# A two-block fp32 transformer kernel: operand order in the matmul blocks, panels that end tile by tile, and new leads behind two norms

## The chip, the cores and the metric

One core of a Trainium2 chip runs the whole program. The metric is the device time of one execution in microseconds (us); lower is better. The engines: TensorE (PE in the profile; PEld is its weight load), VectorE (DVE), ScalarE (ACT), GpSimd (POOL) and the sync engine (SP), which issues the DMAs of the weights.

## What is computed

Two networks follow each other on 256 tokens of width 2048, all in fp32: a block with adaLN modulation, four kinds of attention and a SwiGLU, then two layers with a mixer, a cross-attention to a memory and a layer norm.

```python
def first_block(x, c, ...):
    mod = silu(c) @ ada_w + ada_b                       # sh1, sc1, g1, sh2, sc2, g2
    u = rms_norm(x, g_mix) * (1 + sc1) + sh1
    h = x + g1 * hybrid_mixer(u, w_in, ..., w_out)
    u = rms_norm(h, g_ffn) * (1 + sc2) + sh2
    h = h + g2 * ((silu(u @ w_gate) * (u @ w_up)) @ w_down)
    return rms_norm(h, final_g)

def second_block(h, mem, w_in, w_out, w_mem_kv, ln_g, ln_b, ...):
    for i in range(2):
        u = h @ w_in[i]                                 # i == 1: and h @ w_kv_shared
        mixed = gate(mixer_i(u), memory_attention(u, mem))
        h = layer_norm(ALPHA * h + mixed @ w_out[i], ln_g[i], ln_b[i])
    return h
```

## The kernel before

**Products.** An fp32 product is made of three in the faster format fp32r: with `x = hi + lo` for both operands, `hi*w_hi + hi*w_lo + lo*w_hi`. The activations (`actT`, `hidT`, `mixT`) lie transposed and split in SBUF and are the stationary operand, 128x128 at a time; the weights stream through as the moving one, 512 columns wide. A **block** is one K block of 128 rows of weights for both row tiles of 128 tokens (t = 0, 1): six matmuls, L550 to L552, tile 0's three into one PSUM bank and then tile 1's three into the next:

```python
for t in range(T):
    ...
    nc.tensor.matmul(o, hi, w_hi[:, g, 0:w], ...)
    nc.tensor.matmul(o, hi, w_lo[:, g, 0:w], ...)
    last = nc.tensor.matmul(o, lo, w_hi[:, g, 0:w], ...)
last.then_inc(parts_used, 1)
```

A **panel** is 512 output columns over all K, mostly 16 blocks. The stages in order are `memkv`, `win_k`, `win`, `wout` (first block), `gu0`, `down0`, `gu1`, `down1`, `gu2`, `down2` (SwiGLU), `in0`, `out0`, `in1`, `out1` (the two layers): 1,328 blocks, 7,968 such matmuls.

**Streams.** SP loads pairs of K blocks into a ring `raw` of eight slots and goes on when VectorE has read them (semaphore `blocks_read`). ScalarE rounds a block to `w_hi` (L434) in a ring of `HILO` = 4 slots as soon as TensorE has finished the block four before (`parts_used`); VectorE makes `w_lo = raw - w_hi` (L481) when `hi_ready` says so; TensorE waits for `blocks_read`, that is for `w_lo`, ahead of each block. The order on every engine is written out by hand: `lead`, `hooks`, `at` and `each` are tables from the K block (or a running number) to the other work that is put ahead of this block: attention, accumulation of the adaLN product on VectorE (L460), copies from PSUM.

**Joints.** Where a norm needs all columns of the sum, the last panel of a stage is followed by a chain without products. After `wout`: VectorE multiplies by the gate (`gated_out`, L2142), adds to `X` (L2150), takes statistics (L1944), aggregates and finishes them (`moments`, L1933 to L1938); GpSimd raises to -1/2 (`inv_sqrt`, L1225); ScalarE scales the rows (`normalise`, L1711) by quarters of the width; TensorE transposes them (`turning`, L583; one *turn* is two K blocks, four transposes, eight turns in all, four ahead of the stage and four within it); VectorE scales and shifts (`mod`, L657) into `evac`, ScalarE rounds it to the high part (`high`, L623), VectorE subtracts for the low part (`low`, L664). Meanwhile TensorE runs eleven idle matmuls (`keep_running`, L1348). On VectorE and ScalarE this lead stands behind the first four blocks' `w_lo` and `w_hi` (`in_lead`: `lead[4] = first`), the later turns `g` at K block 2g. After `out0` it is the same with `layer_out` (L2372) and `normalise("l0", X)` in place (L1708). After `out1` comes the end: VectorE subtracts the mean and multiplies by the gain (L2396), then scales and adds the shift (L2400), by halves of the width and row tiles, and SP stores four pieces (L1152).

## Time and profile before

| | |
|---|---|
| median of 3 runs | 2149.55 us (2147.91 to 2149.69) |
| the profiled execution, its own time | 2144.39 us |
| its span, first to last instruction | 2142.7 us |
| mean granted TensorE clock | 0.994 of full speed |
| busy: TensorE, VectorE, ScalarE, GpSimd | 97%, 67%, 50%, 4% |
| DMA over the span | 468.88 MB, 219 GB/s |

The profile is of one execution; its times are its own, and starts are counted from the span's beginning. Matmuls are pipelined and their ends are modelled, so distances between starts say more than their durations. An fp32 transpose or idle matmul is recorded as two passes. In square brackets behind a row stands the idle time of the engine just before it and what ended it.

### The profile page before, as it was taken

The numbers are of one execution on the slowest core, as the hardware profiler recorded it, in microseconds if no ns is written. First come the engines' busy times: TensorE is split into PE (matmuls) and PEld (weight loads), VectorE is DVE, ScalarE is ACT, GpSimd is POOL, SyncE is SP. The second block draws the span as 40 slices with busy tenths as digits, with TensorE's granted clock in tenths as the row PEclk, the third lists the DMA queues.
The fourth block names the chain that finished last, engine by engine and source line by source line (L and its number), as shares of the span: only waits on it lengthen the run. The fifth ranks groups of instructions, "written<-read, shape, count | busy, mean of one in ns | idle before, by whom it ended". The sixth has DMA issues, their size and how long they took to land.

```text
span 2142.7 us, 28517 instructions
## 1 busy us (share of the span) xinstructions
PE 2082.1 (97%) x9926; PEld 1704.7 (80%) x9926; DVE 1428.3 (67%) x2489; ACT 1065.0 (50%) x1955; POOL 86.7 (4%) x156
## 2 busy tenths in 40 slices
PE   6999999999999999999999999999999999999996
PEld 5787788887877887888888888788788788888885
DVE  5987798799577786555555556854455655455556
ACT  3644455555445444445444454454454555555542
POOL 2000011110030000000000000000000000000000
PEclk9999999999999999999999999999999999999998
DMA  8999788888647886666666665664466455555562
GB/s 308 367 366 318 246 289 298 274 292 277 225 157 256 276 291 220 196 194 186 189 191 194 191 187 186 202 211 138 151 214 195 141 156 176 176 160 172 171 225 90
DMA packets 281466, 468.88 MB, mean 219 GB/s; under 512 B 17120, under 2 KB 111552, under 8 KB 279936
## 3 DMA queue, kind: packets, MB, share of 16 engines
q1 hardware_dynamic: 278576, 451.32, 65.1%
q0 software_dynamic: 2768, 15.98, 2.2%
q8 instruction: 71, 1.16, 0.2%
q14 instruction: 51, 0.42, 0.1%
HBM read 465.13 MB, written 2.10 MB: 218 GB/s over the span
## 4 chain that ended last, share of the span: by engine, by line
PE 87%; DVE 5%; issue 5%; ACT 1%; DMA 1%; SPq 0%; POOL 0%; DVEq 0%; POOLq 0%; ACTq 0%
PE ps L550 26%; PE ps L552 25%; PE ps L551 25%; DVE w_lo L481 1%; PE ps L796 1%; PE ps L768 1%; PE ps L1348 1%; PE ps L1633 1%; PE ps L996 1%; PE ps L974 1%; DVE acc_a L460 1%; PE ps L509 1%; PE ps L780 1%; ACT w_hi L434 1%; DMA X<-in_x 1%
## 5 line engine op out<-in xcount | busy, mean ns | idle before, releaser
L481 DVE TENSOR_TENSOR w_lo<-raw,w_hi 128x512 fp32r<-128x512 f32 (+1 forms) x1328 | 901.5, 689 | 646.3 <-ACT w_hi L434 641.2
L434 ACT ACTIVATE w_hi<-raw 128x512 fp32r<-128x512 f32 (+1 forms) x1328 | 830.7, 629 | 989.6 <-PE ps L552 956.3
L550 PE MATMUL ps<-w_hi,actT 128*128 128x512 f32 (+2 forms) x1920 | 771.7, 402 | 11.1 <-DVE w_lo L481 7.1
L552 PE MATMUL ps<-w_hi,actT 128*128 128x512 f32 (+2 forms) x1920 | 747.6, 389 | 0.0
L551 PE MATMUL ps<-w_lo,actT 128*128 128x512 f32 (+2 forms) x1920 | 745.8, 388 | 0.0
L550 PEld LDWEIGHTS ps<-w_hi,actT 128*128 128x128 f32 x1920 | 361.2, 188 | 94.1 <-DVE w_lo L481 10.8
L552 PEld LDWEIGHTS ps<-w_hi,actT 128*128 128x128 f32 x1920 | 361.0, 188 | 76.5
L551 PEld LDWEIGHTS ps<-w_lo,actT 128*128 128x128 f32 x1920 | 361.7, 188 | 69.5 <-issue 1.4
L550 PE MATMUL ps<-w_hi,hidT 128*128 128x512 f32 x352 | 138.4, 393 | 3.0 <-DVE w_lo L481 3.0
L552 PE MATMUL ps<-w_hi,hidT 128*128 128x512 f32 x352 | 137.1, 390 | 0.0
L551 PE MATMUL ps<-w_lo,hidT 128*128 128x512 f32 x352 | 137.0, 389 | 0.0
L550 PE MATMUL ps<-w_hi,mixT 128*128 128x512 f32 x256 | 100.2, 392 | 1.5 <-DVE mixT L2310 1.5
L551 PE MATMUL ps<-w_lo,mixT 128*128 128x512 f32 x256 | 99.6, 389 | 0.0
L552 PE MATMUL ps<-w_hi,mixT 128*128 128x512 f32 x256 | 99.6, 389 | 0.0
L460 DVE SCALAR_TENSOR_TENSOR acc_a<-raw,c_col,acc_a 128x1024 f32<-128x1024 f32 x75 | 97.9, 1305 | 2.1 <-DVE acc_a L460 0.5
L550 PEld LDWEIGHTS ps<-w_hi,hidT 128*128 128x128 f32 x352 | 66.1, 188 | 18.5 <-DVE w_lo L481 2.8
L552 PEld LDWEIGHTS ps<-w_hi,hidT 128*128 128x128 f32 x352 | 66.1, 188 | 13.9
L551 PEld LDWEIGHTS ps<-w_lo,hidT 128*128 128x128 f32 x352 | 66.1, 188 | 13.3
L550 PE MATMUL ps<-w_hi,memT 128*128 128x512 f32 x128 | 52.0, 406 | 12.1 <-DVE memT L614 8.6
L550 PEld LDWEIGHTS ps<-w_hi,mixT 128*128 128x128 f32 x256 | 48.1, 188 | 12.2 <-DVE mixT L2310 2.3
L552 PEld LDWEIGHTS ps<-w_hi,mixT 128*128 128x128 f32 x256 | 48.1, 188 | 10.1
L551 PEld LDWEIGHTS ps<-w_lo,mixT 128*128 128x128 f32 x256 | 48.1, 188 | 9.7
(290 smaller groups left out, 1589.6 us busy)
## 6 DMA issues: line engine op xcount, KB each, us to landing
raw<-in_w_in SPq DMA_DIRECT2D x208, 512.0 KB, 4.5
raw<-in_ada_w SPq DMA_DIRECT2D x192, 512.0 KB, 5.3
raw<-in_w_out SPq DMA_DIRECT2D x96, 512.0 KB, 4.2
raw<-in_ffn_w_gate SPq DMA_DIRECT2D x176, 256.0 KB, 2.9
raw<-in_ffn_w_up SPq DMA_DIRECT2D x176, 256.0 KB, 3.1
...
```

The source lines that it names most:

```text
L434: act.activation(w_hi[:, g, 0:w], raw[:, slot_of(st, it), b, 0:w], ACT.Copy).then_inc(hi_ready, 1)
L460: ins = nc.vector.scalar_tensor_tensor(acc[:, :], both, c_col[:, it.ch:it.ch + 1], acc[:, :], ALU.mult, ALU.add)
L481: nc.vector.tensor_tensor(w_lo[:, g, 0:w], raw[:, slot, b, 0:w], w_hi[:, g, 0:w].bitcast(f32), ALU.subtract).then_inc(blocks_read, 1)
L509: last = nc.tensor.matmul(ps[:, bank, i:i + 1], acc[:, i * P:(i + 1) * P], ones[:, 0:1], start=True, stop=True)
L550: nc.tensor.matmul(o, hi, w_hi[:, g, 0:w], start=first_k, stop=False)
L551: nc.tensor.matmul(o, hi, w_lo[:, g, 0:w], start=False, stop=False)
L552: last = nc.tensor.matmul(o, lo, w_hi[:, g, 0:w], start=False, stop=last_k)
L768: last = nc.tensor.matmul(ps[:, 5 + h, c0:c0 + nk], q[:, t * P:(t + 1) * P], k[:, 0:nk], start=True, stop=True)
L780: last = nc.tensor.transpose(ps[0:self.keys, 5 + h, d:d + P], probs[:, self.par, h, c0 + kt * P:c0 + kt * P + self.keys], ident[:, :])
L796: last = nc.tensor.matmul(o, probsT[0:self.keys, h, d:d + P], self.v(kt, h), start=(kt == 0), stop=(kt == nk // self.keys - 1))
L974: last = nc.tensor.matmul(ps[:, 6 + h, c0:c0 + nk], pair_qkT[:, h, 0, t * P:(t + 1) * P], pair_qkT[:, h, 1, 0:nk], start=True, stop=True)
L996: last = nc.tensor.matmul(o, self.pT[:, h, d:d + P], self.v(kt, h), start=(kt == 0), stop=(kt == nk // P - 1))
```

## The change

- `stage_matmuls`: the six matmuls of a block go by operand: `w_hi` with the high parts of both tiles, `w_hi` with the low parts, then `w_lo` with the high parts. The block now waits for `hi_ready`, and only the fifth matmul for `blocks_read`. With `tiles_apart` (`wout`, `out0`, `out1`) the last four blocks of the last panel are held: all their products for tile 0 come first, then `tile_done`, then all for tile 1.
- VectorE's work behind these three panels goes tile by tile (`last_out`, `layer_out`, `tile_moments`), tile 0's behind `tile_done`.
- Leads of `u2` (into `gu0`) and `h1` (into `in1`): VectorE makes the first two turns' rows itself (`first_rows`); two turns ahead of the stage in place of four, six within it; K blocks 0 and 1 get their high and low parts one by one (`first_hi`, `first_low`). VectorE's lead now stands ahead of its first `w_lo`, and its later steps are `mod(g)` at K block 2g and `low(g)` at 2g + 1. Idle matmuls: 7 and 5 in place of 11 and 11.
- GpSimd builds the pooling masks (`band`) only when the eight turns of `u2` are done. Ahead of `l0`'s `nmean`, `rinv` is signalled.
- The end: tile 0's first half is centred (mean off, gain on) while the panel ends; power for each tile apart; five stores, the last two half as wide (256 KB).

TensorE, one block in a loop (`gu1`), before:

```order
L543 REGISTER_ALU
L550 MATMUL ps<-w_hi,actT 128x512 [waits blocks_read]
L551 MATMUL ps<-w_lo,actT 128x512
L552 MATMUL ps<-w_hi,actT 128x512
L550 MATMUL ps<-w_hi,actT 128x512
L551 MATMUL ps<-w_lo,actT 128x512
L552 MATMUL ps<-w_hi,actT 128x512
```

and with the change:

```order
L559 REGISTER_ALU
L533 MATMUL ps<-w_hi,actT 128x512 [waits hi_ready]
L533 MATMUL ps<-w_hi,actT 128x512 x3
L565 REGISTER_ALU
L533 MATMUL ps<-w_lo,actT 128x512 [waits blocks_read]
L533 MATMUL ps<-w_lo,actT 128x512
```

The two products with `w_lo` have moved behind the other four, and there are two waits in place of one.

VectorE from the norm behind `wout` into `gu0`, before (`evac` is scaling and shifting, `actT` the low part):

```order
L1938 TENSOR_SCALAR ms<-ms 128x2
L481 TENSOR_TENSOR w_lo<-raw,w_hi 128x512 x4
L657 TENSOR_SCALAR evac<-ps,gain,modT 128x256 x4
L664 TENSOR_TENSOR actT<-evac,actT 128x512
L657 TENSOR_SCALAR evac<-ps,gain,modT 128x256 x2
L664 TENSOR_TENSOR actT<-evac,actT 128x512
L481 TENSOR_TENSOR w_lo<-raw,w_hi 128x512 x2
L657 TENSOR_SCALAR evac<-ps,gain,modT 128x256 x2
L664 TENSOR_TENSOR actT<-evac,actT 128x512
L481 TENSOR_TENSOR w_lo<-raw,w_hi 128x512 x2
```

and with the change:

```order
L2009 TENSOR_SCALAR ms<-ms 128x2
L2046 TENSOR_SCALAR xn_68<-X,rinv_x 128x256 x4
L732 TENSOR_SCALAR evac<-ps,gain,modT 128x256 x2
L737 TENSOR_TENSOR actT<-evac,actT 128x256 x2
L481 TENSOR_TENSOR w_lo<-raw,w_hi 128x512 x2
L710 TENSOR_SCALAR evac<-ps,gain,modT 128x256 x2
L481 TENSOR_TENSOR w_lo<-raw,w_hi 128x512
L717 TENSOR_TENSOR actT<-evac,actT 128x512
L481 TENSOR_TENSOR w_lo<-raw,w_hi 128x512
L710 TENSOR_SCALAR evac<-ps,gain,modT 128x256 x2
L481 TENSOR_TENSOR w_lo<-raw,w_hi 128x512
```

The four `w_lo` ahead of the lead are gone from there, the rows are new, and the low part stands between the two `w_lo` of a pair. On ScalarE the high part of a pair still stands ahead of the pair's `w_hi`.

VectorE at the end of the program, before:

```order
L2372 SCALAR_TENSOR_TENSOR X<-X,ps 128x512 x2
L1952 BN_STATS stats<-X 128x6 x2
L1933 BN_AGGR mv<-stats 128x2 x2
L1940 TENSOR_SCALAR ms<-mv 128x2
L2396 SCALAR_TENSOR_TENSOR X<-X,mv,gb_77 128x1024 x2
```

and with the change:

```order
L2502 SCALAR_TENSOR_TENSOR X<-X,ps 128x512
L2028 BN_STATS stats<-X 128x6
L2032 BN_AGGR mv<-stats 128x2
L2517 TENSOR_SCALAR ms<-mv 128x1
L2534 SCALAR_TENSOR_TENSOR X<-X,mv,gb_77 128x1024
L2502 SCALAR_TENSOR_TENSOR X<-X,ps 128x512
```

Tile 0's five steps have moved ahead of tile 1's first. The diff, cut to its core:

```diff
         def stage_matmuls(pe, name, lhs, hooks=None, width=None, as_columns=False, one_acc=False, lead=None, at=None,
-                          sum_at=8, carry=False, each=None):
+                          sum_at=8, carry=False, each=None, tiles_apart=False, between=None):
...
+                held = st.items[-2:] if tiles_apart and (st.bodies == 1 or not first) else []
+
+                def products(it, b, tiles, which):
+
+                    g, kk = (it.g + b) % HILO, 2 * st.place[it.ch] + b
+                    w = width[it.j] if width else NC
+                    first_k, last_k = it is st.first[it.j] and b == 0, it is st.last[it.j] and b == 1
+                    for t in tiles:
+                        last = nc.tensor.matmul(ps[:, bank_of(st, it.j) + t, 0:w], lhs[:, int(which == 1), kk, t * P:(t + 1) * P],
+                                                (w_hi, w_hi, w_lo)[which][:, g, 0:w], start=first_k and which == 0,
+                                                stop=last_k and which == 2)
+                    return last
...
+                        tiles = range(1) if it in held else range(T)
+                        pe.wait_ge(hi_ready, at_p.gb + it.g + b + 1)
+                        products(it, b, tiles, 0)
+                        if between and k in between and first and it.j == 0:
+                            between[k]()
+                        products(it, b, tiles, 1)
+
                         pe.wait_ge(blocks_read, 2 * RING + at_p.kb + it.off + b + 1)
-                        g = (it.g + b) % HILO
-                        for t in range(T):
-                            kk = 2 * st.place[it.ch] + b
-                            hi, lo = (lhs[:, part, kk, t * P:(t + 1) * P] for part in range(2))
-                            first_k, last_k = it is st.first[it.j] and b == 0, it is st.last[it.j] and b == 1
-                            o = ps[:, bank + t, 0:w]
-                            nc.tensor.matmul(o, hi, w_hi[:, g, 0:w], start=first_k, stop=False)
-                            nc.tensor.matmul(o, hi, w_lo[:, g, 0:w], start=False, stop=False)
-                            last = nc.tensor.matmul(o, lo, w_hi[:, g, 0:w], start=False, stop=last_k)
-                        last.then_inc(parts_used, 1)
+                        last = products(it, b, tiles, 2)
+                        if it not in held:
+                            last.then_inc(parts_used, 1)
+                if held:
+                    last.then_inc(S("tile_done"), 1)
+                    for it in held:
+                        for b in range(2):
+                            for which in range(3):
+                                last = products(it, b, (1,), which)
+                            last.then_inc(parts_used, 1)
             run_bodies(pe, st, body)
...
+        def turning_early(pe, src, ready, tag):
+
+
+            def turn(g):
+                ready(g)
+                for i in range(4):
+                    k, t = 2 * g + i // 2, i % 2
+                    last = nc.tensor.transpose(ps[:, 4 + g % 4, i * P:(i + 1) * P], src(k, t), ident[:, :])
+                last.then_inc(turned, 1)
+
+            def taken(g):
+                pe.wait_ge(turn_taken, TURNS[tag] + g + 1)
+
+            def both(g, other):
+                taken(g)
+                turn(other)
+            turn(0)
+            turn(1)
+
+            def second():
+                taken(0)
+                turn(2)
+            n = 1 if tag == "u2" else 3
+            return {0: lambda: pe.wait_ge(S("first_hi"), n), 1: second, 2: lambda: both(1, 3), 4: lambda: both(2, 4), 6: lambda: both(3, 5),
+                    8: lambda: both(4, 6), 10: lambda: both(5, 7), 12: lambda: taken(6), 14: lambda: taken(7)}, {
+                        0: lambda: pe.wait_ge(S("first_low"), n)}
...
+            high = high_of(act, tag, dst)
+
+            def first():
+                n = 2 * ("u2", "h1").index(tag)
+                for k in range(2):
+                    act.wait_ge(S("first_mod"), n + k + 1)
+                    last = act.activation(dst[:, 0, k, :], evac[:, 0, k * SEQ:(k + 1) * SEQ], ACT.Copy)
+                    last.then_inc(S("first_hi"), 1)
+                act.sem_inc(turn_hi, 1)
+                quarter(1)
+                quarter(2)
+                high(1)
+
+            def later(g):
+                if g == 3:
                     quarter(3)
-                high_g(g)
-
-            def first():
-                if quarter:
-                    quarter(0)
-                    quarter(1)
-                high(0)
-                high(1)
-                if quarter:
-                    quarter(2)
-                high(2)
-            return in_lead(first, high)
+                high(g)
+            lead = in_lead(first, later)
+            lead[5] = lambda: high(2)
+            return lead

...
             mod, low = mod_low_of(dve, tag, dst, gain_of, shift_of)

             def first():
-                mod(0)
-                mod(1)
-                low(0)
-                mod(2)
-                low(1)
-
-            def later(g):
-                mod(g)
-                low(g - 1)
-            lead = in_lead(first, later)
-            lead[15] = lambda: low(7)
+                rows_of(0)
+                rows_of(1)
+                n = 2 * ("u2", "h1").index(tag)
+                dve.wait_ge(turned, TURNS[tag] + 1)
+                half = [slice(k * SEQ, (k + 1) * SEQ) for k in range(2)]
+                for k in range(2):
+                    nc.vector.tensor_scalar(evac[:, 0, half[k]], ps[:, 4, half[k]], gain_of(k), shift_of(k), ALU.mult,
+                                            ALU.add).then_inc(S("first_mod"), 1)
+                dve.sem_inc(turn_mod, 1)
+                for k in range(2):
+                    dve.wait_ge(S("first_hi"), n + k + 1)
+                    nc.vector.tensor_tensor(dst[:, 1, k, :], evac[:, 0, half[k]], dst[:, 0, k, :].bitcast(f32),
+                                            ALU.subtract).then_inc(S("first_low"), 1)
+                dve.wait_ge(S("first_low"), n + 2)
+                dve.sem_inc(turn_taken, 1)
+            lead = {2 * g: (lambda g=g: mod(g)) for g in range(1, 8)}
+            lead.update({2 * g + 1: (lambda g=g: low(g)) for g in range(1, 8)})
+            lead[0] = first
             return lead

...
+            pool.wait_ge(turn_taken, TURNS["u2"] + 8)
...
-            stage_matmuls(pe, "wout", actT, each=beside_mixer)
...
-            keep_running(11, 4)
-            lead = turning(pe, "u2", lambda k, t: xn2[:, t, k * P:(k + 1) * P], quarter_ready("u2"))
+            stage_matmuls(pe, "wout", actT, each=beside_mixer, tiles_apart=True)
+
+            keep_running(7, 4)
+            lead, between = turning_early(pe, lambda k, t: xn2[:, t, k * P:(k + 1) * P], quarter_ready("u2"), "u2")
...
+            def tile_moments(q, t, tag):
+
+                ins = v.bn_stats(stats[:, t, q, :], X[:, t, q * NC:(q + 1) * NC])
+                if t == 0:
+                    ins.then_inc(S("tile_stats"), 1)
+                    dve.wait_ge(S("tile_stats"), ("n2", "l0", "l1").index(tag) + 1)
+                    ins = v.bn_aggr(mv[:, 0, :], stats[:, 0, :, :].rearrange("p a b -> p (a b)"))
+                    if tag == "l1":
+                        ins.then_inc(S("tile_mv"), 1)
+                else:
+                    ins.then_inc(S("panel_stats"), 1)
+
+            def first_rows(tag, dst):
+
+                def rows_of(g):
+                    if g == 0:
+                        dve.wait_ge(S("rinv"), NORM[tag])
+                    for t in range(T):
+                        cs = slice(2 * g * P, 2 * (g + 1) * P)
+                        if tag == "n2":
+                            ins = v.tensor_scalar(dst[:, t, cs], X[:, t, cs], rinv_x[:, t:t + 1], None, ALU.mult)
+                        else:
+                            ins = v.tensor_scalar(dst[:, t, cs], X[:, t, cs], mv[:, t, 0:1], rinv_x[:, t:t + 1],
+                                                  ALU.subtract, ALU.mult)
+                    ins.then_inc(S("xn_first"), 1)
+                return rows_of
...
+            def last_out():
+
+                st, cs = ST["wout"], slice(3 * NC, 4 * NC)
+                dve.wait_ge(S("row_taken"), 4)
+                dve.wait_ge(S("panel_stats"), 4 + 3)
+                for t in range(T):
+                    if t == 0:
+                        dve.wait_ge(S("tile_done"), 1)
+                    else:
+                        panel_done(dve, st, 0, 3)
+                    ins = v.tensor_tensor(gy_odd[:, t, :], ps[:, bank_of(st, 3) + t, :], g1_row[:, cs], ALU.mult)
+                    if t == 1:
+                        ins.then_inc(acc_read, 1)
+                        dve.wait_ge(acc_read, 2 + st.end[2])
+                    else:
+                        ins.then_inc(S("tile_gated"), 1)
+                        dve.wait_ge(S("tile_gated"), 1)
+                    v.tensor_tensor(X[:, t, cs], X[:, t, cs], gy_odd[:, t, :], ALU.add).then_inc(S("gy"), 1)
+                    dve.wait_ge(S("gy"), 3 + t + 1)
+                    tile_moments(3, t, "n2")
+            last_out()
...
+                for t in range(T):
+                    if t == 0:
+                        dve.wait_ge(S("natural"), 4 * n)
+                        dve.wait_ge(S("tile_done"), 1 + n)
+                        dve.wait_ge(S("panel_stats"), 4 * NORM[tag] - 1)
+                    else:
+                        panel_done(dve, st, 1, 1)
+                    ins = v.scalar_tensor_tensor(X[:, t, cs], X[:, t, cs], ALPHA, ps[:, bank_of(st, 1) + t, :],
+                                                 ALU.mult, ALU.add)
+                    if t == 1:
+                        ins.then_inc(acc_read, 1)
+                        dve.wait_ge(acc_read, 2 + st.end[2])
+                    else:
+                        ins.then_inc(S("tile_added"), 1)
+                        dve.wait_ge(S("tile_added"), n)
+                    tile_moments(3, t, tag)
+                    if tag == "l1":
+                        if t == 1:
+                            dve.wait_ge(S("panel_stats"), 4 * NORM[tag])
+                            v.bn_aggr(mv[:, 1, :], stats[:, 1, :, :].rearrange("p a b -> p (a b)")
+                                      ).then_inc(S("tile_mv"), 1)
+                        dve.wait_ge(S("tile_mv"), t + 1)
+                        v.tensor_scalar(ms[:, t:t + 1], mv[:, t, 1:2], LN_EPS, None, ALU.add).then_inc(S("ms"), 1)
+                        if t == 0:
+                            while_panel_ends()
+                if tag == "l0":
+                    moments(tag, LN_EPS, False)

...
-                cs = slice(half * D // 2, (half + 1) * D // 2)
-                for t in range(T):
...
-                                           ALU.mult, ALU.add).then_inc(S("y_done"), 1)
+                final(0, slice(half * D // 2, (half + 1) * D // 2))
+            centred(1, slice(0, D // 2))
+            chain(centred(1, slice(D // 2, D)))
+            dve.wait_ge(S("rinv"), NORM["l1"] + 1)
+            for t, cs in OUT_PIECES[2:]:
+                final(t, cs)
```

## Rows read from the trace of the kernel before

**Rows 1.** the page, busy time of each engine
```profile
PE 2082.1 (97%) x9926; PEld 1704.7 (80%) x9926; DVE 1428.3 (67%) x2489; ACT 1065.0 (50%) x1955; POOL 86.7 (4%) x156
```

**Rows 2.** timeline, TensorE in `gu1`: start us, us, engine, line, operation
```profile
1000.54 0.39 PE L551 MATMUL ps<-w_lo,actT 128*128 128x512 f32 x1
1000.77 0.39 PE L552 MATMUL ps<-w_hi,actT 128*128 128x512 f32 x1
1001.00 0.39 PE L550 MATMUL ps<-w_hi,actT 128*128 128x512 f32 x1
```

**Rows 3.** waits of the whole run: us in total, times, longest
```profile
PEld ps L550 <- DVE w_lo L481: 18.3, 24, 2.4
```

**Rows 4.** stretches: us; busy PE, PEld, DVE, ACT, POOL; PEclk, DMA share, GB/s
```profile
55.00:160.00 105.00, 100.88 (x470) 82.69 (x468) 95.26 (x127) 54.93 (x94) 1.09 (x1) 1.00 1.02 366
...
230.00:232.00 2.00, 2.00 (x6) 1.33 (x5) 2.00 (x4) 0.00 (x0) 0.00 (x0) 0.50 0.95 313
...
476.00:515.00 39.00, 34.89 (x231) 29.07 (x229) 38.52 (x105) 23.30 (x69) 3.56 (x3) 1.00 0.81 272
```

**Rows 5.** timeline, TensorE where it waited for `w_lo`
```profile
229.69 0.62 PE L550 MATMUL ps<-w_hi,actT 128*128 128x512 f32 x1 [1.94 <-DVE w_lo L481]
230.11 0.63 PE L551 MATMUL ps<-w_lo,actT 128*128 128x512 f32 x1
...
510.09 0.47 PE L550 MATMUL ps<-w_hi,actT 128*128 128x512 f32 x1 [1.45 <-DVE w_lo L481]
...
1323.93 0.50 PE L550 MATMUL ps<-w_hi,hidT 128*128 128x512 f32 x1 [0.51 <-DVE w_lo L481]
```

**Rows 6.** timeline, the joint from `wout` to `gu0`
```profile
615.78 7.26 PE L1348 MATMUL ps<-cmask,ident 128*128 128x384 f32 x22
...
616.08 1.29 DVE L2142 TENSOR_TENSOR gy_odd<-ps,g_row 128x512 f32<-128x512 f32 x2 [4.18 <-PE ps L552]
...
620.05 0.39 DVE L1933 BATCH_NORM_AGGREGATE mv<-stats 128x2 f32<-128x24 f32 x2
...
620.93 2.49 DVE L481 TENSOR_TENSOR w_lo<-raw,w_hi 128x512 fp32r<-128x512 f32 x4
621.12 1.08 POOL L1225 TENSOR_TENSOR rinv_x<-ms,mhalf 128x2 f32<-128x2 f32 x1 [51.85 <-DVE ms L1938]
...
622.23 2.56 ACT L1711 ACTIVATE xn<-X,rinv_x 128x512 f32<-128x512 f32 x4 [5.63 <-POOL rinv_x L1225]
...
626.92 0.47 PE L550 MATMUL ps<-w_hi,actT 128*128 128x512 f32 x1 [0.98 <-issue]
```

**Rows 7.** timeline, TensorE at `out0`'s end, then one pair of blocks of `in1`
```profile
1674.47 0.48 PE L1348 MATMUL ps<-cmask,ident 128*128 128x384 f32 x1
...
1693.04 0.99 DVE L657 TENSOR_SCALAR evac<-ps,cols 128x256 f32<-128x256 f32 x2
...
1695.25 1.29 DVE L481 TENSOR_TENSOR w_lo<-raw,w_hi 128x512 fp32r<-128x512 f32 x2 [0.62 <-ACT w_hi L434]
1696.46 0.99 DVE L657 TENSOR_SCALAR evac<-ps,cols 128x256 f32<-128x256 f32 x2
...
1694.07 0.63 ACT L623 ACTIVATE actT<-evac 128x512 fp32r<-128x512 f32 x1 [1.75 <-DVE evac L657]
1694.60 1.14 ACT L434 ACTIVATE w_hi<-raw 128x512 fp32r<-128x512 f32 x2
...
1707.81 0.39 PE L550 MATMUL ps<-w_hi,actT 128*128 128x512 f32 x1
```

**Rows 8.** timeline, VectorE behind the last product
```profile
2125.50 1.28 DVE L2372 SCALAR_TENSOR_TENSOR X<-X,ps 128x512 f32<-128x512 f32 x2 [4.15 <-PE ps L552]
...
2129.64 2.48 DVE L2396 SCALAR_TENSOR_TENSOR X<-X,mv,gb 128x1024 f32<-128x1024 f32 x2 [0.91 <-POOL rinv_x L1225]
...
2137.06 2.48 DVE L2400 SCALAR_TENSOR_TENSOR X<-X,rinv_x,gb 128x1024 f32<-128x1024 f32 x2
```

**Rows 9.** the stores of `out`, issue to landing
```profile
DMA to landing us min/median/max: 2.7/2.7/2.7
```

92 lines of the change are left out of this document (49 added, 43 removed).

## The prediction

> **What bounds the kernel now.** The page says TensorE, 97% busy [rows 1]. Matmuls overlap in that row, so I read the distance between starts in the timeline: 0.227 us for a 512-column product, the same when the next one goes to the other row tile and so to another PSUM bank and another stationary block (1000.77 to 1001.00) as when it doesn't (1000.54 to 1000.77) [rows 2]. A block of six takes 1.36 us. Nothing in the change makes it shorter, so the kernel can win only where TensorE waits. There are four kinds of places.
>
> The list of waits gives 18.3 us in 24 waits of the weight load for `w_lo` [rows 3]. The joints behind `wout` and behind `out0`, where a norm needs the whole panel, cost 11.14 us (615.78 to 626.92) and about as much again: fills and transposes, no products [rows 6, 7]. The first 16 blocks behind a joint run slower than 1.36 us, since VectorE has to scale, shift and split the activations beside them [rows 7]. And the tail, from about 2125.2 (0.3 us ahead of the first VectorE step) to the end at 2142.7, is VectorE work [rows 8].
>
> **Order within a block.** The low weights are now used last. A block may start when `w_hi` is there, and needs `w_lo` four products later, 0.91 us. So each wait for `w_lo` shrinks by at most 0.91. Not all of this counts.
> - Before 190 us the DMA share is 1.02 and VectorE is busy for 95.26 of 105 us [rows 4]; eleven adaLN accumulations in a row pace the program there. I take 0 (bound: 2.5 us, as much as three such waits could give).
> - At 229.69 the wait was 1.94 us [rows 5]. It becomes 1.0: gain 0.9. Behind this wait the granted clock is 0.50 [rows 4] and the starts are 0.42 us apart (229.69 to 230.11) [rows 5], which is the 1.2 GHz level. The shorter pause, with four products in its middle, probably keeps 2.4 GHz: six products by 0.2 us are 1.2, and some 0.4 on the 64 small fp32 ones behind them. Gain 1.6, bounds 0 and 3 (twice the price, if a later fall hangs on this one).
> - From 476 to 515 VectorE is busy for 38.52 of 39 us [rows 4]: it paces everything, and the waits (510.09 is the last of three [rows 5]) are one lag. Gain 0.9, bound 2.6.
> - In `down2` three waits of about 0.66 us beyond the pace (1323.93 is the first [rows 5]: 0.51 idle and the slow start behind it) lie 18 us apart. VectorE idles between, so each goes whole: 2.0.
>
> Sum: 5.4. A second wait per block costs nothing as long as it's met: today's wait sits at every sixth product, and the starts don't show it [rows 2]. If the extra wait or the change of bank at every product did cost, it'd be up to 10 ns (the reading error of these starts) by 7,968 products, 80 us. I take 0, since the change of bank is in the rows at no cost and VectorE is normally blocks ahead.
>
> The Trainium skill (TensorE: Matmul & The Clock Gate, "A second HAM failure mode: psum-queue depth-cycling") reports a kernel that cycles through PSUM banks, where TensorE made tiny pauses and its clock went up and down between the two levels. It speaks against switching the bank with every product. With it the sum would turn positive; the last rival prices that from rows.
>
> **The end of a panel ahead of a norm.** Tile 0's share of the last four blocks runs first (12 products), then tile 1's, 2.72 us. VectorE deals with tile 0 under these 2.72 us and has only tile 1 left. Behind `wout` the three pair operations take 3.97 us (616.08 to 620.05) [rows 6]; half goes, and half of the 0.39 aggregation: 2.1 us less. Behind `out0` it is a multiply-add of 1.28 [rows 8], statistics of 1.3 (a third of the 3.97) and the 0.39 aggregation [rows 6]; half is 1.5. The held blocks need all four `w_hi` slots at twice the pace, but those are filled long before: no new wait. The next panel's `w_hi` slots come free as late as today, at the end.
>
> **The lead into the next stage.** Today: power on GpSimd 1.08, first rows on ScalarE 1.3 (half of 2.56), four turns, scaling, high part, low part, first product at E+11.14, E being the end of the last product [rows 6]. Now VectorE writes the first rows itself in quarters of the width (four pieces of 128x256; above nothing, and at most the 0.5 of the scaling form of that size that reads PSUM [rows 7]; I take 0.3), only two turns precede, and K block 0 starts on its high part alone. Behind `out0`, from E: tile 1's chain ends at 2.0, power 3.2, two pieces 3.8, turn 4.5, scale 5.2, high 5.7, first product at **E+5.8**; behind `wout` **E+6.9**. The shorter fills end at E+3.3 and E+4.6, before the first turn; they hide nothing and cost nothing.
>
> So block 0 is 4 to 5 us earlier. But VectorE used to split four `w_lo` blocks (2.49 us) while GpSimd and ScalarE worked [rows 6]; now its lead starts with the rows, and these four come behind. Turn 2 needs ScalarE's rows of the second quarter, which are made after both high halves: block 1 at E+8.4, block 2 at E+11.0 (E+14.0 before).
>
> From there a chain sets the pace. Today two blocks take scale 1693.04, high 1694.07, `w_hi` 1694.60, `w_lo` twice 1695.25, next scale 1696.46: 3.42 us [rows 7], for VectorE leaves the low part of a group to the next one. The new order has the low part between the two `w_lo`: 1.03 + 0.53 + 0.65 + three steps of 0.605 = **4.03 us**, and TensorE waits at the even block for that low part. Its own need is 2.72 and about 0.5 for four transposes. Stepping the three queues through from block 2, six pairs give 3.3 + 3.6 + 4.0 + 4.0 + 3.5 + 4.0 = 22.5: block 14 at E+33.4 behind `out0`. Before it was 1707.81 - 1674.47 = E+33.34 [rows 7]. Behind `wout` the same comes to E+34.4 against E+34.64 (GpSimd's mask work, now moved behind the lead, stretched VectorE by nearly 1 us). **The two joints together give +0.1, which is nothing**: the front gains 5 and the lead pays it back. Bounds: -4 (0.35 us more per pair) and +7 (the old 3.42 us kept).
>
> **The tail.** Before, VectorE from 2125.50 to 2139.54 (2137.06 + 2.48) [rows 8] and then 2.7 us for 512 KB to land [rows 9]. Now tile 0's multiply-add, statistics, aggregation and one 1024-wide centring (1.2) start at E-2.4 and end at E+0.7. Tile 1: 1.8, to E+2.5. Seven more 1024-wide steps by 1.2 and 0.3 of links: E+11.2, against E+14.3. The power on GpSimd (0.9 us of idle before 2129.64 [rows 8]) is now hidden under centring. The last store is half as large: 0.7 less at the rate of the store today. Gain 3.1 + 0.7 = **3.8**, bounds 2.8 and 4.3.
>
> **Sum:** 5.4 + 0.1 + 3.8 = 9.3. The profiled execution took 2144.39 us (span 2142.7) and would take 2135.1. The median of the runs, 2149.55, is 5.2 above it; I carry the difference over: **2140.3**.
>
> **Rivals.**
> 1. *The lead keeps its old pace*: ScalarE's queue or the early start lets TensorE stay ahead, and the 3 to 4 us won at the front of each joint are kept. For: 5 us at block 0 are sure. Against: the 4.03 us are sums of rows. 7 more: 2133.3.
> 2. *The `w_lo` waits only move*: VectorE is all but full up to 515 us [rows 4], and what TensorE wins is lost at the next attention step; the clock falls all the same. Tail and `down2` stay, 5.8, less a lead that is 1 to 2 us worse: 2145.2, within the limit of measurement. That the change does less than it says falls here.
> 3. *Slower: the clock falls in the lead.* Between the shorter fill and block 2 TensorE has some 5 us with pauses of up to 0.8 us and fp32 transposes between; at 229.69 it fell after 1.94 us idle [rows 5]. At 1.2 GHz a block is 2.5 us, a pair with its turn 5.8 instead of 4.03, 12 us per joint if it stays down for seven pairs. It decides from five such pairs in all (9 us). Both joints down: 2140.3 + 25 = 2165. Against: today's joint has a pause of 0.98 us with only transposes ahead of it [rows 6], and the clock holds.
> 4. *The banks.* If 2% of the products ran 0.42 instead of 0.23 us apart [rows 2, 5]: +32 us, 2172. The mean clock is at its upper level for now at a bank change every third product.
>
> **Numbers.** Forecast 0.64, rival 1 0.12, rival 2 0.17, rival 3 0.05, rival 4 0.02. What a measurement can tell from no change is about 0.2%, 4.3 us. Forecast and rival 1 are faster, rival 2 is the same. Range: the forecast's own bounds are 2136 to 2145; taking in rival 1 and rival 2, 2133.5 to 2146.5.
>
> **What would show it.** First products behind the joints at E+6.9 and E+5.8; evacuation steps (`evac`) 4.0 us apart in the lead, not 3.4; block 14 within 1 us of E+34; no wait over 1.1 us at the 229 us place and a granted clock of 1.00 there; `down2` without its three waits; the last VectorE step 11.2 us behind the last product. Wrong if starts within a block are not 0.227 us apart, if the granted clock falls behind E, or if `evac` steps come at 3.4 us.

## The result, and the profile after

| | before | changed |
|---|---|---|
| median of the runs | 2149.62 us (4 runs) | 2136.21 us (4 runs, 2134.53 to 2138.75) |
| ratio, 95% interval | 1 | 0.9944 (0.9927 to 0.9961) |
| profiled execution, its own time | 2144.39 us | 2135.92 us |
| its span | 2142.7 us | 2133.9 us |

The change is faster, by 13.4 us between these medians and by 8.5 us between the two profiled executions. On the chip of the first experiments, with 12 and 23 runs, the medians were 2135.88 and 2144.43, 8.5 us apart, 0.9955 (0.9939 to 0.9970); a 24th run of before, 2676.3 us at a mean clock of 0.741, is left out. The forecast was 9.3 us and 2140.3.

The page of the changed kernel, busy time of each engine; the row answers to [rows 1]. TensorE has the same share, and GpSimd is 8 us busier for one instruction more:

```profile
PE 2079.7 (97%) x9906; PEld 1705.5 (80%) x9906; DVE 1433.7 (67%) x2502; ACT 1062.1 (50%) x1953; POOL 94.8 (4%) x157
```

The waits of the whole run, changed kernel (us, times, longest), against [rows 3]: half as many, but the longest is hardly shorter.

```profile
PEld ps L533 <- DVE w_lo L481: 11.7, 12, 2.2
```

Next I laid both traces side by side by stage. A stage starts at its first weight product; E is the end of the last product ahead of a norm. In us:

| piece | before | before, 2nd trace | changed | changed, 2nd trace |
|---|---|---|---|---|
| start to E of `wout` | 615.78 | 620.77 | 612.59 | 616.41 |
| `gu0` with its lead, and `down0` | 285.86 | 285.90 | 285.91 | 285.98 |
| `gu1` to `gu2` | 397.93 | 397.93 | 397.90 | 397.91 |
| `down2` and `in0` | 285.75 | 285.58 | 282.84 | 282.86 |
| `out0`, lead, `in1` | 450.71 | 450.81 | 451.04 | 451.02 |
| `out1` | 89.20 | 89.16 | 89.19 | 89.16 |
| from there to the end | 17.47 | 17.45 | 14.43 | 14.36 |

**Read the second and fourth columns first.** Behind E of `wout` two executions of one kernel agree within 0.1 us in total (1526.92 and 1526.83; 1521.31 and 1521.29) and within 0.2 in each piece. Ahead of it they differ by 5.0 and 3.8 us. So a single pair of traces decides about everything behind E, and nothing decides about the first 616 us but many runs.

TensorE in the lead of `gu0`, changed kernel; the idle time before a start stands in brackets:

```profile
612.59 4.68 PE L1415 MATMUL ps<-cmask,ident 128*128 128x384 f32 x14
617.34 1.18 PE L625 MATMUL ps<-ident,xn 128*128 128x128 f32 x8
619.13 1.15 PE L533 MATMUL ps<-w_hi,actT 128*128 128x512 f32 x4 [0.61 <-issue]
...
633.45 0.61 PE L533 MATMUL ps<-w_lo,actT 128*128 128x512 f32 x2
634.68 0.66 PE L625 MATMUL ps<-ident,xn 128*128 128x128 f32 x4 [0.62 <-DVE actT L717]
...
637.49 0.61 PE L533 MATMUL ps<-w_lo,actT 128*128 128x512 f32 x2
638.70 0.65 PE L625 MATMUL ps<-ident,xn 128*128 128x128 f32 x4 [0.60 <-DVE actT L717]
```

The first product stands at E+6.54 (forecast E+6.9, before E+11.14 [rows 6]); behind `out0` it is E+5.53 (forecast E+5.8). Pairs of blocks come 4.04 us apart (633.45 to 637.49), each with 0.6 us of waiting for the low part. Block 14 is at E+34.16 and E+33.16; forecast 34.4 and 33.4. VectorE and ScalarE over one such pair show why:

```profile
631.12 0.99 DVE L710 TENSOR_SCALAR evac<-ps,gain,modT 128x256 f32<-128x256 f32 x2
633.33 0.69 DVE L481 TENSOR_TENSOR w_lo<-raw,w_hi 128x512 fp32r<-128x512 f32 x1 [1.22 <-ACT w_hi L434]
633.94 0.68 DVE L717 TENSOR_TENSOR actT<-evac,actT 128x512 fp32r<-128x512 f32 x1
634.54 0.68 DVE L481 TENSOR_TENSOR w_lo<-raw,w_hi 128x512 fp32r<-128x512 f32 x1
635.15 0.99 DVE L710 TENSOR_SCALAR evac<-ps,gain,modT 128x256 f32<-128x256 f32 x2
...
632.15 0.63 ACT L672 ACTIVATE actT<-evac 128x512 fp32r<-128x512 f32 x1 [2.35 <-DVE evac L710]
632.68 1.14 ACT L434 ACTIVATE w_hi<-raw 128x512 fp32r<-128x512 f32 x2
```

In each such pair VectorE is idle for 1.22 us and ScalarE for 2.35, each waiting for the other: `w_hi` needs nothing of this pair, but stands behind the high part, which waits for the scaling step. That was the pace of 4.03 us in the prediction, and here is also its cure.

### The profile page after: what moved, and what is told of

It is laid out like the page before. It is cut to its first block, busy times and chain, and to the rows that moved or that the text cites. A ratio compares the mean times of both kernels' runs of the same rounds, so it can differ in the third digit from the quotient of the medians.

```text
span 2133.9 us, 28754 instructions
## 1 busy us (share of the span) xinstructions
PE 2079.7 (97%) x9906; PEld 1705.5 (80%) x9906; DVE 1433.7 (67%) x2502; ACT 1062.1 (50%) x1953; POOL 94.8 (4%) x157
## 4 chain that ended last, share of the span: by engine, by line
PE 91%; DVE 6%; ACT 1%; issue 1%; DMA 1%; SPq 0%; POOL 0%; DVEq 0%; ACTq 0%
PE ps L533 80%; DVE w_lo L481 2%; PE ps L856 1%; PE ps L828 1%; PE ps L1415 1%; PE ps L1701 1%; PE ps L1056 1%; PE ps L1034 1%; DVE acc_a L460 1%; PE ps L840 1%; PE ps L509 1%; ACT w_hi L434 1%; DVE ada_acc L493 1%; DMA raw<-in_w_mem_kv 1%; PE ps L1470 0%
## 5 line engine op out<-in xcount | busy, mean ns | idle before, releaser
L533 PE MATMUL ps<-w_hi,actT 128*128 128x512 f32 (+2 forms) x3840 | 1053.4, 396 | 4.3 <-DVE actT L717 3.2
L533 PE MATMUL ps<-w_lo,actT 128*128 128x512 f32 (+2 forms) x1920 | 592.3, 389 | 5.1 <-DVE w_lo L481 5.1
L533 PE MATMUL ps<-w_hi,hidT 128*128 128x512 f32 x704 | 189.6, 391 | 0.0
L533 PE MATMUL ps<-w_hi,mixT 128*128 128x512 f32 x512 | 138.9, 390 | 1.5 <-DVE mixT L2428 1.5
L533 PE MATMUL ps<-w_lo,hidT 128*128 128x512 f32 x352 | 108.6, 390 | 0.5 <-DVE w_lo L481 0.5
L533 PEld LDWEIGHTS ps<-w_hi,memT 128*128 128x128 f32 x256 | 48.4, 192 | 18.8 <-issue 9.0
L493 DVE SCALAR_TENSOR_TENSOR ada_acc<-raw,c_col,ada_acc 128x512 f32<-128x512 f32 x60 | 45.9, 766 | 1.1
L1319 POOL TENSOR_SCALAR tab<-dist 128x384 f32<-128x384 f32 (+1 forms) x34 | 33.8, 999 | 192.0 <-DVE sm L915 191.3
L533 PE MATMUL ps<-w_lo,memT 128*128 128x512 f32 x128 | 40.5, 398 | 1.6 <-DVE w_lo L481 1.4
L460 DVE SCALAR_TENSOR_TENSOR acc_d<-raw,c_col,acc_d 128x1024 f32<-128x1024 f32 x30 | 40.3, 1343 | 0.8 <-DVE acc_d L457 0.5
```

The source lines that it names most:

```text
L460: ins = nc.vector.scalar_tensor_tensor(acc[:, :], both, c_col[:, it.ch:it.ch + 1], acc[:, :], ALU.mult, ALU.add)
L493: nc.vector.scalar_tensor_tensor(acc, raw[:, slot, b, :], c_col[:, k:k + 1], acc, ALU.mult, ALU.add).then_inc(blocks_read, 1)
L533: last = nc.tensor.matmul(ps[:, bank_of(st, it.j) + t, 0:w], lhs[:, int(which == 1), kk, t * P:(t + 1) * P], (w_hi, w_hi, w_lo)[which][:, ...
L1319: last = g.tensor_scalar(to, of, -val / SC, 1.0, ALU.mult, ALU.mult)
```

## The experiments

Twelve kernels ran, two of them without an edit. Ratios are to the kernel before on the same chip.

| kernel | median us | ratio (95%) |
|---|---|---|
| after_again | 2135.88 | 0.9955 (0.9939 to 0.9970) |
| order_only | 2136.89 | 0.9964 (0.9950 to 0.9978) |
| order_and_tiles | 2133.41 | 0.9946 (0.9924 to 0.9969) |
| tiles_short_fills | 2132.53 | 0.9937 (0.9911 to 0.9963) |
| high_later | 2131.54 | 0.9934 (0.9910 to 0.9958) |
| small_spread | 2131.69 | 0.9926 (0.9902 to 0.9950) |
| pause_filled | 2135.65 | 0.9953 (0.9933 to 0.9973) |
| scale_split | 2129.10 | 0.9924 (0.9898 to 0.9950) |
| all_mended | 2119.33 | 0.9876 (0.9853 to 0.9898) |
| before_again, masks_back, masks_in_down0 (one run each) | 2149.32, 2135.68, 2121.74 | |

### The parts of the change, and its leads

**after_again**: no edit.

> The changed kernel itself, so that the parts can be compared on one chip. Theory 1 (the whole gain is waits, joints and tail, as the two profiled executions show: 3.2 us up to the end of wout, 2.9 more up to the end of out0, 3.0 in the tail): 8 to 10 us below the kernel before. Theory 2 (the profiled execution of before was a quick one, and runs differ in the first 515 us, where the DMA share is about 1): 12 to 14 us below.

**order_only**: the diff of `stage_matmuls` alone, without `tiles_apart`.

> The kernel before with the new order of operands alone (high weights with both parts, then low weights, with the two waits). Theory 1 (the wait for w_lo shrinks or goes up to 515 us and in down2, nothing else): 4 to 6 us faster than before, the joints as before (block 14 of gu0 34.6 us behind the end of wout). Theory 2 (the w_lo waits only move): within 2 us of before. Theory 3 (changing the PSUM bank with every product costs): slower.

**order_and_tiles**: this, with tile-by-tile panels and the new end; leads, fills and masks as before.

> The new order of operands, the panels that end tile by tile and the new end of the program, with the old leads, the old fills and GpSimd's masks where they were. Theory 1 (the new leads give their early start back): equal to the whole change within 2 us: the first product of gu0 comes 9 us behind the end of wout and not 6.5, but block 14 about 32.5 us behind it, better than the 34.2 of the whole change. Theory 2 (the new leads are worth their early start of 3 to 4 us per joint): 4 to 8 us slower than the whole change.

Behind E of `wout` the traces give 1526.92 us before, 1523.07 with the order alone, 1518.72 with tiles and end too, 1521.31 for the whole change. The order is worth 3.85 there: 2.5 in `down2`, 0.4 in `in0`, and 1.0 at the start of `down0`. Its median is 7.5 us under before, where 4 to 6 was expected; some 3.7 of it lies ahead of E. The end is worth 3.0. The rest of the change, the leads with their fills and the masks, is **2.6 us slower** than the old leads behind the same panels. So theory 1 on order_and_tiles holds in sign, but its numbers don't: the first product came at E+10.37 and not E+9, block 14 at E+33.8 and not 32.5.

**tiles_short_fills**, on order_and_tiles:

```diff
-            keep_running(11, 4)
+            keep_running(7, 4)
...
-            keep_running(11, 4)
+            keep_running(5, 4)
```

> The kernel with new order and tile-by-tile panels but old leads, now with 7 and 5 idle matmuls in place of 11 and 11. Theory 1 (eleven fills keep TensorE for 7.26 us behind the end of wout and hold the first turn, so that only 0.8 and 0.5 us of the earlier norm arrived): first products at about 9.0 us behind wout (10.37 with the long fills) and 9.3 behind out0 (10.34), 2 to 2.4 us less in all. Theory 2 (the first turn waits for ScalarE's rows anyway): no change. A fall of the granted clock in the lead would speak for a third, that the long fills were needed: 5 us or more slower.

The same place, TensorE in order_and_tiles:

```profile
609.58 7.26 PE L1372 MATMUL ps<-cmask,ident 128*128 128x384 f32 x22
616.68 1.91 PE L605 MATMUL ps<-ident,xn 128*128 128x128 f32 x16
619.95 1.15 PE L533 MATMUL ps<-w_hi,actT 128*128 128x512 f32 x4 [1.36 <-issue]
```

and in tiles_short_fills:

```profile
612.32 4.68 PE L1372 MATMUL ps<-cmask,ident 128*128 128x384 f32 x14
618.14 2.32 PE L605 MATMUL ps<-ident,xn 128*128 128x128 f32 x16 [1.15 <-ACT xn L1735]
621.44 0.93 PE L533 MATMUL ps<-w_hi,actT 128*128 128x512 f32 x3 [0.98 <-issue]
```

With eleven fills the transposes start as the fills end, with no idle time: the fills had become the bound. With seven they wait for ScalarE's rows. First products moved to E+9.12 and E+9.67, the part behind E to 1516.88: 1.8 us less, 4.4 us better than the whole change. Behind `wout` the clock stayed at 1.00. Behind `out0`, with five fills, the fall of the third theory showed in this trace, though not its 5 us:

```profile
1671.37 3.43 PE L605 MATMUL ps<-ident,X 128*128 128x128 f32 x16 [2.78 <-ACT X L1732]
...
1672.00:1673.00 1.00, 1.00 (x7) 0.91 (x6) 0.72 (x2) 0.73 (x2) 0.00 (x0) 0.50 0.88 324
```

Behind an idle time of 2.78 us the granted clock (third column from the end) was 0.50 for some 3.5 us, into the transposes, and the first product came at E+9.67 and not E+9.3. None of the other thirteen traces shows a fall there, also not the changed kernel's with the same five fills in its shorter lead. The number of fills belongs to its lead: too many delay it, too few can, by this one trace, cost the clock.

**high_later**, on the changed kernel: on ScalarE the high part goes behind the pair's first `w_hi`.

```diff
-            def later(g):
-                if g == 3:
-                    quarter(3)
-                high(g)
-            lead = in_lead(first, later)
-            lead[5] = lambda: high(2)
+            lead = {2 * g + 1: (lambda g=g: high(g)) for g in range(2, 8)}
+            lead[4] = first
+            lead[6] = lambda: quarter(3)
```

> The whole change, but on ScalarE the high part of turn g (2 to 7) stands behind the first w_hi of its pair and not ahead of it (and the last quarter of the rows ahead of K block 6). Theory 1 (the 4.02 us per pair in the lead is the chain scale, high part, w_hi, w_lo, low part, w_lo; with w_hi made earlier VectorE no longer idles 1.22 us per pair): the scaling steps come 3.3 us apart, block 14 at 30.6 us behind the end of wout (34.2 in the changed kernel) and 29.7 behind out0 (33.2), 7 us faster than the whole change. Theory 2 (a slot of the ring or the transposes set the pace): the steps stay 4.0 us apart, no gain.

VectorE, then TensorE, in high_later:

```profile
632.50 0.99 DVE L707 TENSOR_SCALAR evac<-ps,gain,modT 128x256 f32<-128x256 f32 x2
633.40 0.69 DVE L481 TENSOR_TENSOR w_lo<-raw,w_hi 128x512 fp32r<-128x512 f32 x1
634.19 0.69 DVE L714 TENSOR_TENSOR actT<-evac,actT 128x512 fp32r<-128x512 f32 x1
634.80 0.69 DVE L481 TENSOR_TENSOR w_lo<-raw,w_hi 128x512 fp32r<-128x512 f32 x1
635.40 0.99 DVE L707 TENSOR_SCALAR evac<-ps,gain,modT 128x256 f32<-128x256 f32 x2
...
632.70 0.60 PE L625 MATMUL ps<-ident,xn 128*128 128x128 f32 x4
633.05 1.18 PE L533 MATMUL ps<-w_hi,actT 128*128 128x512 f32 x4
...
635.90 0.60 PE L625 MATMUL ps<-ident,xn 128*128 128x128 f32 x4
```

No brackets are left: VectorE takes 2.90 us per pair (3.3 was expected) and TensorE its own 3.20. Block 14 is at E+29.93 and E+28.93, 4.2 us earlier at each joint; behind E of `wout` 1512.52, **8.8 us** less than the changed kernel. The median shows 4.3 of it; its six runs had a mean clock of 0.9915 (0.9926 in after_again), and its trace had 615.08 ahead of E, where the edit changes nothing.

### GpSimd's masks, and the start of `down0`

The leads gained 0.34 us by block 16 and `down0`'s start about 1.0, yet `gu0` with `down0` is no shorter. I looked for the missing 1.4.

**masks_back**, on the changed kernel:

```diff
-            pool.wait_ge(turn_taken, TURNS["u2"] + 8)
```

> The whole change, but GpSimd builds the pooling masks without waiting for the eight turns of u2. Theory 1 (behind the lead the masks slow VectorE down and cost 1.4 us in gu0, seen as waits for w_lo of 0.5 and 0.2 us at 57 and 60 us behind the end of wout): those waits go; VectorE's steps in the lead stretch, one pair takes 0.5 to 1 us longer, and gu0 with down0 takes 0.4 to 0.9 us less than the 285.9 of the changed kernel. Theory 2 (the masks are free behind the lead and the 1.4 us have another cause): the waits stay, gu0 with down0 takes up to 1 us longer.

**masks_in_down0**, on high_later; the last adaLN row also goes behind `down0`'s second `w_lo`:

```diff
-            pool.wait_ge(turn_taken, TURNS["u2"] + 8)
+            pool.wait_ge(ada_taken, 1 + ST["gu0"].end[3])
```

> The kernel with high parts behind the first w_hi, and the masks on GpSimd only once the adaLN rows are all added (the start of down0), and this last addition behind down0's second w_lo. Theory 1 (the masks cost 1.4 us in gu0 as long as they run beside its full VectorE, and nothing in down0; the wait of 1.0 for w_lo at the start of down0 is that addition): gu0 and down0 together 279.2 us (281.6 with the high parts later alone, 285.9 in the changed kernel), no wait for w_lo at 57 to 60 us behind wout or at down0's start. Theory 2 (masks cost the same wherever they are): 280.6.

The changed kernel, 57 us behind E of `wout`, GpSimd, VectorE, TensorE:

```profile
664.10 6.86 POOL L1357 TENSOR_TENSOR band<-band,ident 128x128 f32<-128x128 f32 x8
...
666.22 1.82 DVE L481 TENSOR_TENSOR w_lo<-raw,w_hi 128x512 fp32r<-128x512 f32 x2
667.96 1.82 DVE L493 SCALAR_TENSOR_TENSOR ada_acc<-raw,c_col,ada_acc 128x512 f32<-128x512 f32 x2
...
670.70 0.73 PE L533 MATMUL ps<-w_lo,actT 128*128 128x512 f32 x2 [0.48 <-DVE w_lo L481]
```

and VectorE in masks_in_down0 at the same place of the program:

```profile
657.03 1.29 DVE L481 TENSOR_TENSOR w_lo<-raw,w_hi 128x512 fp32r<-128x512 f32 x2
658.24 1.53 DVE L493 SCALAR_TENSOR_TENSOR ada_acc<-raw,c_col,ada_acc 128x512 f32<-128x512 f32 x2
```

Two `w_lo` take 1.82 us beside the masks and 1.29 without, two accumulations 1.82 and 1.53. The Trainium skill (GPSIMD Engine Reference, "1. Specifications") says that GpSimd's way to SBUF is shared with VectorE, whose instructions with two SBUF inputs contend with it; both forms here have two, and the trace agrees. In masks_back the waits in `gu0` go (1.4 us back), but the lead grows by 1.8 (block 16 at E+38.80 in place of E+37.02): 286.32 in all, 0.4 more than the changed kernel and not less, so theory 1 had the mechanism and the wrong balance. In masks_in_down0 the sum is 279.42 (expected 279.2), 2.2 less than high_later: 1.45 for the masks, 0.75 for the start of `down0`. **Moving the masks behind the lead was right, and not far enough.**

### The clock ahead of E

**before_again**: no edit.

> The kernel before once more, for a second trace of its first 616 us, which differ from run to run. Theory 1 (the granted clock falls once or twice there, at a different phase in each run, and the rest of the program is fixed): the time from the end of wout to the end of the span is again 1526.9 us within 0.3, and all of the difference lies ahead of it, with the share of time at the lower clock. Theory 2 (the whole program varies): the part behind wout differs by more than 1 us.

Theory 1 held: 1526.83 behind E. Ahead of it 620.77, with two long falls of the granted clock between 227 and 254 us. In 23 runs of before on one chip, time goes with the mean granted clock: spans of 2148.1 to 2150.2 us at 0.990 (seven runs), 2142.1 to 2143.8 at 0.993 (eight), 2136.1 to 2138.2 at 0.996 (three).

Stretches of the changed kernel; columns: us, busy time (count) of PE, PEld, DVE, ACT, POOL, granted clock, DMA share, GB/s:

```profile
224.00:227.00 3.00, 2.33 (x22) 1.97 (x23) 3.00 (x7) 0.63 (x1) 0.00 (x0) 0.81 0.91 301
227.00:230.00 3.00, 3.00 (x31) 3.00 (x31) 2.42 (x4) 0.00 (x0) 0.00 (x0) 0.50 0.91 250
...
491.00:494.00 3.00, 3.00 (x13) 2.96 (x13) 2.96 (x19) 0.47 (x1) 0.00 (x0) 0.50 0.93 329
```

At 224 us the wait for `w_lo` is 1.79 us, not the 1.0 forecast, and the clock falls as before [rows 4, 5]. At 491 it falls where the trace before keeps 1.00. Both were put to a test.

**small_spread**, on the changed kernel: the two groups of 64 small products that follow the wait go in six parts ahead of six K blocks.

```diff
-                for j in range(CMP_LEN):
+                for j in range(11 * part, min(11 * part + 11, CMP_LEN)):
...
-                elif n in (9, 11):
-                    cmp_hidden((n - 9) // 2)
+                elif 7 <= n < 13:
+                    cmp_hidden((n - 7) // 3, (n - 7) % 3)
```

> The whole change, but the two groups of 64 small products (64x64 by 30 columns, some 4 us each at the upper clock) are given out in six thirds ahead of six K blocks, so that no 4 us pass without full blocks. Theory 1 (the clock falls there because of these small products, with or without the wait for w_lo of 1.8 us ahead of them): no stretch with a granted clock of 0.5 between 225 and 250 us, 4 to 5 us faster than the changed kernel, mean clock 0.995. Theory 2 (the wait alone makes it fall): it still falls once for 3 to 10 us behind the wait, gain under 2 us.

**pause_filled**: the changed kernel with three idle matmuls in the wait, the small products as they were.

```diff
                         products(it, b, tiles, 1)
+                        if name == "win" and st.n0 + it.g + b == 8:
+                            for _ in range(3):
+                                nc.tensor.matmul(ps[:, 4, 0:384], ident[:, :], cmask[:, :], start=True, stop=True)
```

> The changed kernel with three idle matmuls (0.66 us each) between the fourth product of K block 8 of win and its wait for w_lo, so that TensorE works through the wait of 1.8 us ahead of the small products, which stay in two groups of 64. Spreading these groups took away the falls of the granted clock and the wait alike; this run parts the two. Theory 1 (the small products make the clock fall): the wait is gone from TensorE's rows, and the clock still falls to 0.5 within 10 us, at least one fall of 3 us or more between 224 and 250 us; mean clock 0.992 to 0.994, time as the changed kernel within 1.5 us. Theory 2 (the wait makes it fall): no granted clock under 1.00 between 222 and 236 us, a mean clock of 0.995 or more, 3 to 5 us faster.

small_spread, the same view:

```profile
227.00:230.00 3.00, 3.00 (x32) 2.42 (x30) 3.00 (x7) 0.58 (x2) 0.00 (x0) 1.00 0.95 319
```

pause_filled, TensorE and then the view by stretches:

```profile
222.35 2.10 PE L566 MATMUL ps<-cmask,ident 128*128 128x384 f32 x6
224.31 0.73 PE L533 MATMUL ps<-w_lo,actT 128*128 128x512 f32 x2
224.98 4.69 PE L1473 MATMUL ps<-cmp_in,w_k 64*64 64x30 f32 x64
...
235.33 4.78 PE L1473 MATMUL ps<-cmp_in,w_v 64*64 64x30 f32 x64
...
227.00:230.00 3.00, 3.00 (x34) 2.94 (x33) 2.05 (x3) 0.00 (x0) 0.00 (x0) 0.64 0.99 300
230.00:233.00 3.00, 3.00 (x10) 2.31 (x10) 0.00 (x0) 0.44 (x1) 0.00 (x0) 0.50 0.98 349
...
239.00:242.00 3.00, 3.00 (x16) 2.55 (x16) 0.00 (x0) 0.00 (x0) 0.00 (x0) 0.50 0.06 21
```

With the products spread, every stretch from 224 to 245 us has 1.00, and so it is in the two other traces with this edit. The time from the start of `win_k` to the first 480-column panel is 254.79 us (259.04 and 261.77 in the two traces of the changed kernel), and six runs have mean clocks of 0.995 and 0.996. But the wait had gone as well.

With the wait filled instead, TensorE is busy for all of every stretch and the clock still falls twice, from 227.8 and from 238.1 us, each time 2.8 us into a group of small products; the second group has neither a wait nor an idle matmul right ahead of it. The median is 2135.65 (on a chip where before took 2144.57), so nothing was gained. So the small products (64x64 weights, 30 columns, 4 us in a row) can make the clock fall by themselves, though not each time: the changed kernel's second group, at 237.24, ran at 1.00. The place at 380 us is of the same kind: 28 short products take 3.5 us there without a wait, and in six of the fourteen traces the clock is 0.50 for 3.4 us from about their end on.

By the traces the wait can do it too. Before, the starts are 0.42 us apart from 229.69 on, right behind the wait [rows 5], and the first small product comes only at 232.38; in before_again, order_only and tiles_short_fills too the fall begins ahead of the small products. So filling the wait doesn't help while the small products stand behind it. The other half, small products spread and the wait kept, was not run. The Trainium skill (TensorE: Matmul & The Clock Gate, "Why this matters for your kernels") advises keeping idle gaps between bursts short. Here the clock fell with no gap in pause_filled.

**scale_split**, on small_spread: two scaling steps on VectorE, 1.23 and 1.29 us in a row from 483.58 us on, right behind an accumulation of 1.28 and ahead of one `w_lo`, are parted: the first moves one K block ahead, with a `w_lo` between them. (The 2.5 in the expectations is both steps together.)

```diff
-                elif n == 132:
+                elif n == 131:
                     subnorm_scale()
+                elif n == 132:
+                    subnorm_gain()
```

> The changed kernel with the small products spread, and VectorE's two scaling steps at 487 us (3.7 us in a row) parted by one w_lo. Theory 1 (the new order gathered the lag into one wait of 1.13 us in the middle of a block, and behind this wait the granted clock falls to 0.5 for some 5 us, which the kernel before did not show): the wait falls below 0.5 us, no granted clock under 1.00 from 476 to 515, that stretch 1.5 to 2 us shorter, 25.7 or less in place of 27.3. Theory 2 (the fall has to do with the short products of the attention there): the wait goes and the clock falls all the same.

In the changed kernel:

```profile
486.60 0.55 PE L533 MATMUL ps<-w_lo,actT 128*128 128x320 f32 x2 [1.14 <-DVE w_lo L481]
487.08 0.63 PE L828 MATMUL ps<-qkT 64*128 64x16 f32 x8
```

In scale_split:

```profile
491.00:494.00 3.00, 3.00 (x24) 2.74 (x23) 3.00 (x7) 1.07 (x4) 0.00 (x0) 1.00 0.93 333
```

This wait is gone, no stretch from 140 to 620 us is under 1.00, and the 27.3 us from the first 320-column panel to `wout` became 25.08. But `wout` itself took 0.8 longer, and TensorE now waits elsewhere: 1.48 us for ScalarE's `proj` at 475.78 and 1.01 us for `w_lo` at 499.45, inside `wout`. The gain also depends on what it is held against. In five of the ten traces with the new order and the old scaling the fall lasts 3.4 us and not 6.8, and then the same stretch takes 25.7 us and `wout` 0.3 longer, which leaves the edit 0.1 us; against the long fall it is 1.4. Theory 1 fits in that wait and fall went together, but the cause isn't shown: before has a wait of 1.71 us there without a fall, all ten traces with the new order and a wait of 1.1 have one, and scale_split's own 1.48 and 1.01 bring none.

### All together

**all_mended** joins high_later, masks_in_down0 and scale_split, with one `w_lo` ahead of VectorE's rows (`lead[1] = first`).

> The whole change with all that the earlier runs point to: high parts behind the pair's first w_hi (4.1 and 4.4 us fewer per joint), one w_lo ahead of the rows on VectorE, the small products in six thirds, the masks on GpSimd during down0, the last row of the adaLN product added behind down0's second w_lo, and VectorE's scaling of the differential heads (1.2 + 2.5 us in a row ahead of one w_lo at 487 us) in two pieces with a block between. Theory 1 (these are separate costs that add): behind the end of wout 1509.9 us (1521.3 in the changed kernel), ahead of it 607 (612.6), so a span of 2117 and 15 to 18 us faster than the changed kernel, 24 to 28 faster than before. Theory 2 (what is won ahead is lost to the next wait, as between operand order and clock): under 12 us faster than the changed kernel.

Its span is 2117.7 us: 607.16 ahead of E (expected 607; scale_split's one trace had 604.10), 1510.54 behind (expected 1509.9). The median is 2119.33, 16.6 us under the changed kernel's 2135.88, which was measured on another chip (before took 2145.35 and 2144.43 on the two), and 1.2% under before on its own. The `w_lo` ahead of the rows gained nothing: block 16 at E+32.51 (32.65 in high_later) and E+31.98 (31.65).

## Why the prediction was right, and where it was not

Behind E of `wout` the span fell by 5.61 us, forecast 5.9 (2.0 + 0.1 + 3.8). Ahead of E by 3.19 in the pair of profiled executions, forecast 3.4. The total lies close, 8.5 us of time and 8.8 of span against 9.3, but its second part is in part luck: the two second traces differ there by 4.36, and the medians leave 2.9 us for it where they are 8.5 apart and 7.8 where they are 13.4 apart. Of the terms these hold and fail:

- **Nothing within a block.** Held: where nothing waits, blocks start 1.36 us apart in the new order too, as here in `out1` (changed kernel, TensorE):

```profile
2109.95 1.07 PE L533 MATMUL ps<-w_hi,mixT 128*128 128x512 f32 x4
2110.86 0.62 PE L533 MATMUL ps<-w_lo,mixT 128*128 128x512 f32 x2
2111.31 1.07 PE L533 MATMUL ps<-w_hi,mixT 128*128 128x512 f32 x4
```

  Rival 4, the change of bank, is refuted: with a switch at every product the clock stayed at 1.00 from 650 us to the last product. The Trainium skill (TensorE: Matmul & The Clock Gate, "A second HAM failure mode: psum-queue depth-cycling") tells of small pauses that came with cycling through banks. No such pauses showed here, so the switch by itself brought nothing of the kind. (Rival 4's price was a little off too: 2% of 7,968 products, each 0.19 us later, is 31 us and not 32.)
- **The joints, +0.1.** Held: block 16 comes 0.34 us earlier behind `wout` and 0.01 behind `out0`. The lead gave back 4.3 and 5.3 us of front. Behind `out0` the chain ran as worked out: block 2 at E+10.55 (forecast 11.0), the six pairs in 22.6 us (forecast 22.5, though its own six terms add up to 22.4). Rival 1 is out, and rival 3 too: the clock shows 1.00 from 614 to 650 us and from 1680 to 1720.
- **`down2`, 2.0.** It was 2.5, and 0.4 more in `in0`.
- **The end, 3.8.** It was 3.04. VectorE's part, to E+11.2 (E is 2119.47, 0.23 behind the last product's start), is exact. The 0.7 for a smaller last store was wrong: no store landed sooner than 2.7 us after its issue, as before [rows 9]. VectorE's last steps and the stores, changed kernel:

```profile
2128.05 2.61 DVE L2537 SCALAR_TENSOR_TENSOR X<-X,rinv_x,gb 128x1024 f32<-128x1024 f32 x3
...
DMA to landing us min/median/max: 2.7/2.7/2.8
```

  I had scaled a time that did not scale with size here; whether the store ahead of it delayed it wasn't tried.
- **The early terms, 3.4.** The sum came near without its reasons, and this is the step that failed. The wait at the 229 us place went from 1.94 to 1.79 and not to 1.0. The wait of 0.47 us at 224.73 has gone, and so both together went from 2.41 to 1.79: the order saved 0.62 of the 1.38 (0.47 + 0.91) that it could save at these two, and the rest was waited for at the second, as rival 2 says. The clock fell all the same (1.6 forecast): pause_filled shows that a shorter or filled pause doesn't save it while 64 small products follow. From the first 320-column panel to `wout` it was 0.13 of the 0.9, a new fall eating the rest: there rival 2 was right too. What made up the 3.19 in this pair stood elsewhere: 2.4 in `memkv`, where I had taken 0 with a bound of 2.5, and 1.8 from `win_k` to the first 480-column panel, less 1.2 for a fall at 380 us that the first trace of before doesn't have and the second has. `memkv` took 100.9 and 100.0 us before and 97.7 to 100.6 in the twelve traces with the new order, so its gain varies from execution to execution.
- **Missed: two terms that cancel.** The wait of 1.47 us ahead of `down0`'s first product was one of the 24 of [rows 3] and I gave it no term (gain 1.0). And I priced the masks only where they left, not where they went (loss 1.4).
